# The row maximum of an attention score tile taken in two pieces: 1024 keys once two of the tile's three parts have landed, 256 at the end

## The reference

```python
def attend(q_nope, q_rope, k_nope, k_rope, v):
    s = (jnp.einsum("bqhd,bkhd->bhqk", q_nope, k_nope)
         + jnp.einsum("bqhr,bkr->bhqk", q_rope, k_rope))
    p = jax.nn.softmax(s.astype(jnp.float32) * ATTN_SCALE, axis=-1).astype(v.dtype)
    return jnp.einsum("bhqk,bkhd->bqhd", p, v)
```

## Time and profile before

| | us |
|---|---|
| median of 3 runs | 2524.23 (2520.44 to 2526.75) |
| the profiled execution, its time | 2521.44 |
| the profiled execution, its span | 2520.1 |
| PE busy in it | 2442.8 (97%) |
| DVE busy | 1293.4 (51%) |
| ACT busy | 674.3 (27%) |
| POOL busy | 300.2 (12%) |

### The profile page before, as it was taken

The page is one execution under the profiler, slowest core; times in us unless marked ns, Lnnn a source line. Parts: engine busy times, 40 slices in busy tenths (PEclk is TensorE's granted clock), DMA queues, the critical chain, the costliest instruction groups (busy, mean ns, idle before and its releaser), DMA issues.

```text
span 2520.1 us, 28557 instructions
## 1 busy us (share of the span) xinstructions
PE 2442.8 (97%) x11405; PEld 2018.2 (80%) x11405; DVE 1293.4 (51%) x1904; ACT 674.3 (27%) x1026; POOL 300.2 (12%) x183
## 2 busy tenths in 40 slices
PE   6889999999999999999999999999999999999998
PEld 4678888888778888888888788888788888888887
DVE  7667777786664333333444663255743333334444
ACT  5245554453432122221212421112311111101112
POOL 4211112100411111111100200001100000000002
PEclk9899999999999999999999999999999999999998
DMA  7001111123222222222211120121111111111111
GB/s 277 32 24 41 40 48 48 40 76 115 79 93 82 92 88 88 86 90 92 92 59 59 42 65 28 42 67 34 34 51 50 49 44 43 51 50 50 50 34 67
DMA packets 48047, 163.30 MB, mean 65 GB/s; under 512 B 5184, under 2 KB 6592, under 8 KB 47808
## 3 DMA queue, kind: packets, MB, share of 16 engines
q1 hardware_dynamic: 47936, 161.72, 19.5%
HBM read 157.51 MB, written 4.19 MB: 64 GB/s over the span
## 4 chain that ended last, share of the span: by engine, by line
PE 90%; DVE 6%; ACT 1%; POOL 1%; DMA 1%; issue 1%; SPq 0%; ACTq 0%; DVEq 0%; POOLq 0%
PE ps L481 25%; PE ps L483 25%; PE ps L482 25%; PE ps L865 3%; PE ps L799 1%; PE ps L801 1%; PE ps L803 1%; PE ps L800 1%; PE ps L804 1%; PE ps L844 1%; PE ps L846 1%; PE ps L845 1%; DVE h_lo L1886 1%; DVE tmp L1879 1%; DVE x L1712 1%
## 5 line engine op out<-in xcount | busy, mean ns | idle before, releaser
L481 PE MATMUL ps<-h_hi,w_hi 128*128 128x512 f32 x1792 | 701.5, 391 | 15.1 <-DVE h_lo L1886 15.1
L482 PE MATMUL ps<-h_lo,w_hi 128*128 128x512 f32 x1792 | 698.8, 390 | 0.0
L483 PE MATMUL ps<-h_hi,w_lo 128*128 128x512 f32 x1792 | 698.8, 390 | 0.0
L1906 DVE TENSOR_TENSOR ab<-ab,ps 128x512 f32<-128x512 f32 x88 | 60.5, 688 | 733.8 <-PE ps L483 714.3
L481 PEld LDWEIGHTS ps<-h_hi,w_hi 128*128 128x128 f32 x1792 | 337.2, 188 | 90.1 <-DVE h_lo L1886 20.6
L483 PEld LDWEIGHTS ps<-h_hi,w_lo 128*128 128x128 f32 x1792 | 337.3, 188 | 70.6
L482 PEld LDWEIGHTS ps<-h_lo,w_hi 128*128 128x128 f32 x1792 | 337.4, 188 | 69.3
L1712 DVE SCALAR_TENSOR_TENSOR x<-ps,mods,x 128x512 f32<-128x512 f32 x448 | 325.5, 748 | 103.5 <-PE ps L483 84.7
L481 PE MATMUL ps<-g_hi,w_hi 128*128 128x512 f32 x832 | 325.2, 391 | 3.8 <-DVE x L1712 2.8
L482 PE MATMUL ps<-g_lo,w_hi 128*128 128x512 f32 x832 | 323.7, 389 | 0.0
L483 PE MATMUL ps<-g_hi,w_lo 128*128 128x512 f32 x832 | 323.7, 389 | 0.0
(11 more groups left out here) (258 smaller groups left out, 2699.5 us busy)
## 6 DMA issues: line engine op xcount, KB each, us to landing
raw<-stream SPq DMA_DIRECT2D x172, 512.0 KB, 3.6
mod_raw_f<-ada_rows SPq DMA_DIRECT2D x48, 512.0 KB, 4.8
mod_raw<-ada_rows SPq DMA_DIRECT2D x32, 512.0 KB, 3.5
ada_ring<-ada_pe SPq DMA_DIRECT2D x16, 512.0 KB, 12.8
x<-x_t SPq DMA_DIRECT2D x8, 512.0 KB, 8.1
out_t<-x SPq DMA_DIRECT2D x16, 256.0 KB, 2.0
hraw<-head_w SPq DMA_DIRECT2D x8, 384.0 KB, 3.0
x0a<-x_t SPq DMA_DIRECT2D x2, 1024.0 KB, 6.3
```

The lines of the kernel that those rows point to most:

```text
L481: nc.tensor.matmul(out, w[0][wi], a[0][ai], start=start, stop=False)
L482: nc.tensor.matmul(out, w[0][wi], a[1][ai], start=False, stop=False)
L483: return nc.tensor.matmul(out, w[1][wi], a[0][ai], start=False, stop=stop)
L1906: nc.vector.tensor_tensor(ab[unit % 2][:], ab[unit % 2][:], ps[:, 2 * (unit % 2) + 1, :], ALU.mult)\
```

## The change

`M j` becomes two items. `N j` stands right behind part 3j+1: DVE waits for a new semaphore, `s_top`, that PE sets with that part's last matmul, and takes the maximum of those 1024 keys (`row_max_most`). `M j` stays behind part 3j+2: it takes the maximum of the last 256 keys, and the scaling instruction joins the two. `N` stands at steps 7, 0, 2 and 4 (behind S1, S4, S7, S10), `M` at 8, 1, 3 and 5. In the last pass's last group there are no scores, so 15 of the 16 groups carry the four pairs, and with the tiles ahead of the loop there are 64 pairs. PE's and ACT's instructions stay as they are and in their order.

```diff
@@ group_script
         for n in PARTS_AT[k]:
             out.append(("S", group, n))
-            if n % 3 == 2:
-                out.append(("M", group, n // 3))
+            if n % 3:
+                out.append(("M" if n % 3 == 2 else "N", group, n // 3))
@@ FIRST_ITEMS
-                [("S", 0, n)] + ([("M", 0, n // 3)] if n % 3 == 2 else [])
+                [("S", 0, n)] + ([("M" if n % 3 == 2 else "N", 0, n // 3)] if n % 3 else [])
...
-               + [("S", 1, 0), ("S", 1, 1), ("S", 1, 2), ("M", 1, 0), ("T", 0, 0), ("X", 1, 0), ("S", 1, 3),
+               + [("S", 1, 0), ("S", 1, 1), ("N", 1, 0), ("S", 1, 2), ("M", 1, 0), ("T", 0, 0), ("X", 1, 0), ("S", 1, 3),
@@ scores_part
+            if part == 1:
+                last.then_inc(s_top, 1)
             if part == 2:
                 last.then_inc(s_mm, 1)
@@ DVE
+        def row_max_most(j):
+
+            C.add("s_top")
+            dve.wait_ge(s_top, C.at("s_top"))
+            first = 0 if j % 2 == 0 else TK + TC
+            own(nc.vector.tensor_reduce(mx_raw[:, 2 + j % 2:3 + j % 2], flat[:, first:first + T], AX_X, ALU.max))
+
         def row_max(j):
             C.add("s_mm")
             dve.wait_ge(s_mm, C.at("s_mm"))
-            own(nc.vector.tensor_reduce(mx_raw[:, j % 2:j % 2 + 1], flat[:, TK * (j % 2):TK * (j % 2 + 1)], AX_X,
-                                        ALU.max))
-            nc.vector.tensor_scalar(nmax[:, j % 2:j % 2 + 1], mx_raw[:, j % 2:j % 2 + 1], -SCALE, None, ALU.mult)\
-                .then_inc(mx, 1)
+            at = j % 2
+            own(nc.vector.tensor_reduce(mx_raw[:, at:at + 1], flat[:, T + TC * at:T + TC * (at + 1)], AX_X, ALU.max))
+            nc.vector.tensor_scalar(nmax[:, at:at + 1], mx_raw[:, at:at + 1], mx_raw[:, 2 + at:3 + at], -SCALE,
+                                    ALU.max, ALU.mult).then_inc(mx, 1)
```

More of the change, by code:

```diff
@@ L321, in build @@
     rinv = sb("rinv", [8], F32, 2656)
-    mx_raw = sb("mx_raw", [2], F32, 2688)
+    mx_raw = sb("mx_raw", [4], F32, 2688)
     bias_sb = sb("bias_sb", [PRO_TILES, 2], F32, 2720)
@@ L434, in build @@
         sem(n) for n in "kv_sq q_sq q_acc kr_t kr_sh kr_rot kv_done kr_done q_done tok_t tok_h tok_done".split())
-    hw_h, hw_l, uv_h, uv_l, rg, ra, rd, s_mm, mx, ex, ri, pv, ol_r, ol_l, q_sh, q_rot, q_ready = (
-        sem(n) for n in "hw_h hw_l uv_h uv_l rg ra rd s_mm mx ex ri pv ol_r ol_l q_sh q_rot q_ready".split())
+    hw_h, hw_l, uv_h, uv_l, rg, ra, rd, s_mm, s_top, mx, ex, ri, pv, ol_r, ol_l, q_sh, q_rot, q_ready = (
+        sem(n) for n in "hw_h hw_l uv_h uv_l rg ra rd s_mm s_top mx ex ri pv ol_r ol_l q_sh q_rot q_ready".split())
     o_h, sil, gm, cs, zm, gl, fin = (sem(n) for n in ("o_h", "sil", "gm", "cs", "zm", "gl", "fin"))
@@ L1788, in item @@
         def item(kind, gb, k):
-            if kind == "M":
+            if kind == "N":
+                row_max_most(k)
+            elif kind == "M":
                 row_max(k)
@@ L1863, in _ @@
         with dve.Fori(0, passes) as i:
-            C.enter(i, {"ra": RING_PASS, "s_mm": 16, "ex": 16, "hw_h": 2, "uv_h": 2, "q_rot": 4, "pv": 40, "ol_r": 4,
-                        "v": 16 + 4 + 4 + 6, "in_mod0": 64, "in_mod1": 64, "mod_out": 1})
+            C.enter(i, {"ra": RING_PASS, "s_mm": 16, "s_top": 16, "ex": 16, "hw_h": 2, "uv_h": 2, "q_rot": 4, "pv": 40, "ol_r": 4,
+                        "v": 2 * 16 + 4 + 4 + 6, "in_mod0": 64, "in_mod1": 64, "mod_out": 1})
             for gb in range(4):
```

## The result

| | before, us | after, us |
|---|---|---|
| median of 4 runs | 2524.22 (2520.44 to 2526.75) | 2550.44 (2547.69 to 2552.16) |
| the profiled execution, its time | 2521.44 | 2552.16 |
| its span | 2520.1 | 2550.8 |

The ratio is 1.0098, with a 95% interval of 1.0084 to 1.0113: 26.2 us more by the medians, where 2550 had been forecast and 27.5 us more by the sum.

The account below looks back on a forecast made before the run. PE was taken to be full in the loop, so an earlier maximum could only be free or cost. Terms 16.9 + 3.5 + 4.2 + 2.0 + 1.4 - 0.1 - 0.4 = 27.5 us gave 2550 us, range 2538 to 2560.

Parts of the forecast that it names:

- What bounds the kernel: In the loop PE is busy 339.99 of 340.00 us, so shortening DVE's or ACT's work can give nothing there.
- The price of a piece: On DVE: 1.22 us for 1024 keys and 0.43 for 256, so a pair costs 0.2 us more than before.
- Term 1: Step 2 to 3, every group: `B` waits for the diagonals, 1.04 us in nine groups, 1.25 in six; 16.9 us.
- Term 2: Steps 4 to 7, six even loop groups and the last pass's first: `PV 7` starts 0.50 us late; 3.5 us.
- Term 3: Step 8, six odd groups of the loop: `Q 1` waits for `qa_lo`, 0.70 us each; 4.2 us.
- The small terms: PE restarts at 22 places cost 2.0 us, register instructions at 28 places 1.4; the start gives 0.1, the last pass 0.4.
- more than 0.05 us after the piece: Sign that the forecast is too low: the reciprocal at step 2 starts later than this behind the first piece.
- The sum: Whole kernel: all terms together 27.5 us slower, 2548.9 by the profiled execution's time, given as 2550.
- Only the diagonals stall: Rival: only `B` waits, later chains at `PV 7` and `Q 1` meet unseen slack; 18 us, 2541; chance 0.11.
- Every first piece costs more: Rival: register instruction costs 0.13 us at all 28 places, piece nearer 1.35 us; 6 more, about 2557; chance 0.08.
- The first piece hides: Rival: the piece fits idle DVE time, decided at `B`; not slower, 2519.4 to 2523.5; chance 0.07.

Follow-up runs that it names:

- e5: Changed kernel with three of each group's four first pieces moved behind the work that was late, tile 1's left early; 2526.36 us, 1.0002 of the kernel before.
- e6: Changed kernel with only tile 2 of each group split, all other tiles and those ahead of the loop whole; 2540.59 us, 1.0059 of the kernel before.
- e9: Changed kernel with only tile 3 of each group split, all other tiles whole; one execution, 2526.39 us beside 2527.18 for the kernel before.
- e10: Changed kernel with only tile 0 of each group split, all other tiles whole; one execution, 2529.52 us beside 2527.18 for the kernel before.
- e8: Changed kernel with pieces in the groups alone, the five tiles ahead of the loop whole; 2552.55 us, 1.0103 of the kernel before.
- e2: Changed kernel with both pieces of each maximum together behind the third part, where the single maximum stood; 2527.65 us, 1.0012 of the kernel before.
- e3: Changed kernel without DVE's own wait for the end of the first piece; 2546.32 us, 1.0090 of the kernel before.
- e7: Changed kernel with pieces only in the tiles ahead of the loop, whole maxima in the groups; 2526.35 us, 1.0000 of the kernel before.
- e4: Changed kernel with first pieces of 512 keys and last pieces of 768, at the same places; 2535.03 us, 1.0045 of the kernel before.
- e1: Changed kernel with only the first piece for S7 moved behind the reciprocal and the diagonals; 2536.95 us, 1.0054 of the kernel before.

## Why the prediction was right, step by step

**What bounds the kernel.** "No shortening of DVE's work can give anything there; the change can only be free or cost" held: e5 is free, and no version with pieces in the groups is faster. "Nothing waits on PE's side" was a little too strong, as the sum shows.

**The price of a piece.** 1.216 us for the 1.22 taken from two subtractions, 0.413 for 0.43. The four sizes measured, 256, 512, 768 and 1024 keys, with 413, 682, 947 and 1216 ns lie on a line of 1.045 ns an element, with 146 ns fixed. The Trainium skill's formula ("VectorE: DVE Perf Modes", The TRN2 errata) gives estimates of 1.19 and 0.39, some 0.02 too little for each; the trace decides. A fixed cost for each instruction is there, and it isn't what this change loses by.

**Term 1, the diagonals.** Right in mechanism and nearly in size. From the start of S8's last matmul to the first product behind `B`, so that `B`'s own restart is in it, the trace of before has 0.93 us in even groups and 1.06 in odd ones. After, it has 2.15 in group 0, 2.06 in group 2, 2.31 in the odd groups and 1.97 in the last pass: later by 1.22, 1.13, 1.25 and 1.04. With 3, 3, 6 and 3 groups that is 17.7 us. The forecast, with restart (0.09) and register instruction (0.05), was 1.18 for nine groups and 1.30 for six, 18.4: 0.7 too high, half of it in the last pass, which I priced like the even groups; there `B` starts 0.05 behind the diagonals and not 0.13. e6's stretch has 17.0 and not 17.7, for a reason that the sum had left out: in the kernel before PE comes late at two transposes, by 0.2 us in the loop (270.62) and 0.45 in the last pass (533.17), because of a low part, and when PE is later already, this lateness is gone.

**Term 2, `PV 7`.** Seven waits, idle for 0.44 us in group 0 and 0.37 or 0.38 in the others, for 0.50; from start to start 0.68 on average, 4.7 in all, where 0.50 + 0.09 + 0.05 = 0.64 had been forecast. e9's stretch is 4.3 us longer, and the forecast for it was 4.1 (3.5, with 0.6 for restarts, 0.4 for register instructions, less 0.4 at the end).

**Term 3, `Q 1`.** Alone it was sized well: +5.3 us in e10, 0.89 us for each of 6, where 0.70 + 0.09 + 0.05 = 0.84 had been forecast. In the changed kernel it waits for only 0.3 us each, where alone it waited 0.6: from start to start it comes 0.55 us later than before, 3.3 us in all for the 5.0 of the forecast. This term was mis-sized by 1.7 us. The step that failed is one that I hadn't written out: that the modulation row ahead of `pt_lo` of tile 9 ends where it ended before, seen from PE. The row of group 1, step 7, in the traces of before, of after and of e10, with GpSimd's instructions around it:

```profile
211.83 1.30 POOL L2143 TENSOR_TENSOR qsb<-qsb,qsh 128x512 f32<-128x512 f32 x1
212.37 1.84 DVE L1814 SCALAR_TENSOR_TENSOR mod_raw<-mod_raw,row_a 128x1024 f32<-128x1024 f32 x1
213.09 2.28 POOL L2139 TENSOR_TENSOR qsb<-qsb,tab 128x512 f32<-128x512 f32 x1
```

```profile
219.78 1.28 POOL L2154 TENSOR_TENSOR qsb<-qsb,qsh 128x512 f32<-128x512 f32 x1
220.53 1.61 DVE L1825 SCALAR_TENSOR_TENSOR mod_raw<-mod_raw,row_a 128x1024 f32<-128x1024 f32 x1
221.03 2.27 POOL L2150 TENSOR_TENSOR qsb<-qsb,tab 128x512 f32<-128x512 f32 x1
```

```profile
213.79 1.29 POOL L2164 TENSOR_TENSOR qsb<-qsb,qsh 128x512 f32<-128x512 f32 x1
213.95 2.21 DVE L1835 SCALAR_TENSOR_TENSOR mod_raw<-mod_raw,row_a 128x1024 f32<-128x1024 f32 x1
215.04 2.27 POOL L2160 TENSOR_TENSOR qsb<-qsb,tab 128x512 f32<-128x512 f32 x1
```

The row takes 1.22 us where GpSimd is idle. Here it takes 1.84, 1.61 and 2.21, but in each of the three it ends 1.08 us after the end of GpSimd's sum that was running when it started (213.13 to 214.21, 221.06 to 222.14, 215.08 to 216.16). So GpSimd sets the end of the row. GpSimd works on what DVE's shuffles of the query give it, and the first of these stands behind the maximum of tile 3 in DVE's queue. Before, it starts 0.09 us behind the scaled maximum (208.30 and 208.39, group 1), in three of the six groups up to 0.44 behind it; after, the maximum is through sooner and DVE stands idle for 0.49 us until the shuffle's own input is there. So GpSimd starts sooner beside PE's work, and the row ends sooner. Over the six odd groups the row takes 1.83 to 2.23 us before and, with tile 3 whole, in e6 and e10; it takes 1.56 to 1.62 after, in e8 and in e9, where tile 3 is split. Means over six groups are 1.95 before and 1.58 after, 2.2 us in all, near the 1.9 by which `Q 1` is later in e10 than in the changed kernel (5.2 and 3.3). e2 shows the other direction: there the maximum of tile 3 is through 0.25 us later than before, the shuffle starts 0.03 behind it, and the row takes 2.01 to 2.08. The shorter last piece pays back part of term 3. The link from the maximum to GpSimd is read from the traces, and e2, e6, e9 and e10 bear it out; no run changed GpSimd's work by itself.

**The small terms.** Behind the piece 0.03 us of gap and 0.05 for the register instruction had stood in the sum, 0.08 together. In the trace the next instruction starts 0.12 us behind the piece at 15 of the 28 places (the diagonals of group 0, and `PV 7` and `Q 1` in the loop) and 0.03 at the other 13: 0.08 on average. So the sign "more than 0.05 us after the piece" came in part, and it didn't push the sum up. e3's 0.17 a place is more, since without the wait the instructions overlap by 0.07. At the end of the last pass the wait of 1.32 us became 0.38 and that of 0.34 behind it stayed, but the product ahead of them (`PV 7` of group 2), which didn't wait before, now waits 0.33; from start to start PE gains 0.36 there, for the 0.4 taken. At the start the wait for the exponential grew by 0.5 us, where 0.2 had been taken.

**The sum.** 27.6 forecast for the stretch, 24.96 measured. Term 1 is 0.7 below its forecast, term 3 1.7 below, term 2 0.2 above, and the 0.7 of the two late transposes had no term; the rest, 0.3 us, is spread over places that I can't name. That 2550 came within 0.4 us of the median is in part luck: by the sum on the median of before it should have been 2551.7, and the interval of the measured ratio is 3.6 us wide to either side. The median comes 26.2 us over that of before, the two profiled executions differ by 30.7 in span: 25.0 in the stretch, 0.7 behind it, and 5.0 ahead of it. 2.4 of these lie before the first changed instruction. The other 2.6 lie at the start (first score part to the stretch: 39.37 us before, 41.93 after), where the granted clock was 0.83 and not 0.96. With whole maxima at the start, that clock was 0.96 in before, e9 and e10 and 0.79 in e6 and e8; with split ones it was 0.79 (e7), 0.83 (after, e4, e5) and 0.87 (e1, e2, e3). So it varies without any change of the pieces; but 0.96 was seen with whole maxima alone, and the profiles by themselves don't exclude that the pieces bear on it. What speaks against a cost is e7's median, equal to that of before.

**The rivals.** *Only the diagonals stall* (2541) falls: in e6 only the diagonals stall, its time is 2540.59, and the changed kernel's is 9.9 above it. The changed kernel's own trace has the waits at `PV 7` and `Q 1` besides. *Every first piece costs more* falls with 1.216 us and with the gap of 0.08 behind it. *The first piece hides* falls at `B`, as priced; e5 shows what it would have been worth if it hid, nothing.

## What to carry to other kernels

In a queue that runs in order, starting a piece of work early moves it ahead of all that stood between its old and its new place. Before such a split, find for each new place the next instruction that another engine waits for, and its slack: here nothing to 0.3 us at `B`, some 0.7 at `PV 7` and 0.5 at `Q 1` stood against a piece of 1.2. Put the early piece behind that instruction, and check the one after it too, or leave it whole; and where the waiting engine is already full, as PE was, expect nothing from an earlier result even if it comes free.

## What the runs showed that I had not expected

DVE's multiplication of a modulation row (both operands in SBUF) and GpSimd's sums hold each other up: the row takes 1.22 us alone and up to 2.23 behind a running GpSimd instruction, and GpSimd's next instruction takes 2.27 us for its 1.29. The Trainium skill says as much ("SBUF — State Buffer", Who interferes with whom: a DVE instruction with two inputs in SBUF contends with a GpSimd instruction that reads SBUF, and the port pair that they share is an exclusive lock), and the trace agrees: the row ends 1.08 us after GpSimd's end each time.

The small scaling instruction takes 60 ns more (154 to 214) with an operand read from memory in place of a constant, and a maximum in front of the multiplication; which of the two costs it, no run separates. A wait for the end of the instruction just issued cost the work behind it, which doesn't need it, 0.17 us. And the start of before and of e8, both with whole maxima, took 39.4 us at a granted clock of 0.96 and 43.4 at 0.79: 4 us that a single profile can put down to a change wrongly.
